# Sample attention of a hybrid decoder step: cached keys turned on VectorE in 32x32 blocks, scores as 32x64 products on eight array tiles, value product moved into the merge

## What is computed

```python
def latent_attention(q_lat, q_rope, c, kr, q_pos, k_pos):
    s = (jnp.einsum('bqhr,bkr->bhqk', q_lat, c)
         + jnp.einsum('bqhp,bkp->bhqk', q_rope, kr)).astype(jnp.float32) * ATTN_SCALE
    s = jnp.where(k_pos[None, :] <= q_pos[:, None], s, -jnp.inf)
    pr = jax.nn.softmax(s, axis=-1).astype(c.dtype)
    return jnp.einsum('bhqk,bkr->bqhr', pr, c)
...
    o = jnp.einsum('bthr,rhv->bthv', o_lat, w_kv[..., QK_NOPE:]).reshape(b, t, MLA_HEADS * V_HEAD)
    y_b = o @ p['w_branch_b']
```

## Time and profile before

| what | value |
|---|---|
| median of 3 runs | 2714.29 us (2712.4 to 2716.27) |
| profiled execution | span 2723.1 us, first to last instruction; no other time of it is recorded |
| PE busy, DVE busy, ACT busy in that span | 92%, 67%, 50% |
| prompt attention ends, sample attention starts | about 251 us |
| first product of the merge | 551.61 us |

### The profile page before, as it was taken

The page is one execution under the profiler, slowest core; times in us unless marked ns, Lnnn a source line. Parts: engine busy times, 40 slices in busy tenths (PEclk is TensorE's granted clock), DMA queues, the critical chain, the costliest instruction groups (busy, mean ns, idle before and its releaser), DMA issues. The chain is left out here.

```text
span 2723.1 us, 35695 instructions
## 1 busy us (share of the span) xinstructions
PE 2506.0 (92%) x12991; PEld 1924.5 (71%) x12991; DVE 1834.4 (67%) x2157; ACT 1354.4 (50%) x1417; POOL 454.7 (17%) x367
## 2 busy tenths in 40 slices
PE   8798999888996999997988899999999999999994
PEld 5355555588994454447976778888888888888883
DVE  0344444343774676563445689999999999999997
ACT  0243322132332454343223377777777777777774
POOL 0001122000001232220011522222111222222211
PEclk9899999898997898898998899999999999999997
DMA  4102344132224134304253699999999999999995
GB/s 145 69 1 99 102 170 155 39 98 77 79 63 138 30 122 126 89 11 112 82 164 131 193 387 396 396 381 381 380 382 382 384 380 376 384 378 378 380 377 183
DMA packets 242307, 585.41 MB, mean 215 GB/s; under 512 B 25632, under 2 KB 114976, under 8 KB 237728
## 3 DMA queue, kind: packets, MB, share of 16 engines
q1 hardware_dynamic: 225176, 508.42, 51.1%
q0 software_dynamic: 17024, 75.53, 9.2%
HBM read 548.10 MB, written 35.67 MB: 214 GB/s over the span
## 5 line engine op out<-in xcount | busy, mean ns | idle before, releaser
L2406 DVE TENSOR_TENSOR w_lo<-w_raw,w_hi 128x2048 fp32r<-128x2048 f32 x291 | 660.2, 2289 | 60.6 <-ACT w_hi L2356 53.8
L2356 ACT ACTIVATE w_hi<-w_raw 128x2048 fp32r<-128x2048 f32 x288 | 550.4, 1916 | 137.7 <-PE banks L2299 102.5
L2299 PE MATMUL banks<-w_hi,x_hi 128*128 128x512 f32 x1024 | 319.9, 394 | 2.4 <-DVEq L2445 2.1
L2299 PE MATMUL banks<-w_lo,x_hi 128*128 128x512 f32 x1024 | 317.0, 391 | 0.0
L2299 PE MATMUL banks<-w_hi,x_lo 128*128 128x512 f32 x1024 | 316.6, 391 | 0.0
L2406 DVE TENSOR_TENSOR w_lo<-mergedT,w_hi 128x2048 fp32r<-128x2048 f32 x96 | 220.1, 2292 | 38.0 <-ACT w_hi L2356 37.9
L2299 PEld LDWEIGHTS banks<-w_hi,x_lo 128*128 128x128 f32 x1024 | 192.9, 188 | 41.0
L2299 PEld LDWEIGHTS banks<-w_lo,x_hi 128*128 128x128 f32 x1024 | 192.8, 188 | 40.8
L2299 PEld LDWEIGHTS banks<-w_hi,x_hi 128*128 128x128 f32 x1024 | 190.7, 189 | 40.5 <-DVEq L2445 2.1
L2356 ACT ACTIVATE w_hi<-mergedT 128x2048 fp32r<-128x2048 f32 x96 | 183.8, 1915 | 34.4 <-PE banks L2299 29.7
L2259 POOL DMA_INDIRECT y_sum<-xT,to_row x32 | 50.9, 1590 | 858.1 <-ACT xT L2388 858.1
(11 more groups left out here) (460 smaller groups left out, 4724.2 us busy)
## 6 DMA issues: line engine op xcount, KB each, us to landing
w_raw<-in_exp_w_gu SPq DMA_DIRECT2D x196, 1024.0 KB, 10.7
w_raw<-in_exp_w_down SPq DMA_DIRECT2D x96, 1024.0 KB, 6.4
mergedT<-in_exp_w_gu SPq DMA_DIRECT2D x64, 1024.0 KB, 10.3
mergedT<-in_exp_w_down SPq DMA_DIRECT2D x32, 1024.0 KB, 10.1
w_x<-in_w_in SPq DMA_DIRECT2D x11, 1024.0 KB
out<-h SPq DMA_DIRECT2D x20, 512.0 KB, 2.6
wz<-in_w_in SPq DMA_DIRECT2D x4, 2048.0 KB, 11.6
dec<-acs_rows SPq DMA_DIRECT2D x16, 512.0 KB, 4.1
```

The source lines that it names most:

```text
L2299: mm = pe.matmul(banks[:, bank + c, :], x[:, k, :], part[:, s % NHI, j, c * 512:(c + 1) * 512], start=start, stop=last)
L2356: act.activation(w_hi[:, s % NHI], raw(s, par), ACT.Copy).then_inc(hi_ready, 1)
L2406: dve.tensor_tensor(w_lo[:, s % NHI], raw(s, par), w_hi[:, s % NHI].bitcast(F32), ALU.subtract).then_inc(lo_ready, 1)
```

## The change

- **Keys.** The 20 PE transposes of a unit and their five copies go. DVE turns the keys itself, in 32x32 blocks, from the ring to `keyT` in SBUF: per unit two transposes of 1024 columns (latent features) and one of 512 (rotary). In `keyT` partition 32i + x then holds feature x of a block of 32 features, for the keys of partition group i.
- **Scores.** A 32-feature block is multiplied by itself: 32 rows of the array (group i) by 64 columns (half c) make a product with 256 keys. Ten blocks, two halves, four groups give 80 products for two units, which now form one step (`PAIRS` = 16 steps). The group i writes to PSUM bank i. The queries must lie on all four groups: SP writes them to DRAM in the stage before (`q_rows`) and reads them back four times per sequence (`q4`).
- **Softmax.** No score copy: DVE takes the maximum of a step from PSUM, ACT takes the exponent from PSUM, with a running maximum and a factor `alpha` that rescales the first step of a sequence when the second is added (`gather`).
- **Pipeline.** One step is behind the scores instead of five units. The ring has nine places, two of which are lent by `wkv`, whose value half SP loads again at the end of the stage.
- **End.** The two halves are added on DVE, with ACT moving one half across partitions; the product with the value half of `wkv` stands in `stage_merge`, where DVE's copies to `oT` come between its `tile_low`.
- **POOL** clears five small tiles after its second unit.

```diff
+            @block.sync
+            def _(sp):
+                sp.wait_ge(prep_out, 4 * HEADS)
+                by_rank = io.q_rows.rearrange("b r j q -> r j b q")
+                for j in range((KVL + ROPE) // 32):
+                    at = slice(32 * (j % 4), 32 * (j % 4) + 32)
+                    q = sb.qlS[at, j // 4] if j < 8 else sb.qrS[at]
+                    sp.dma_start(by_rank[:, j], q.rearrange("p b h t -> p b (h t)")).then_inc(q_put, 16)
+                sp.wait_ge(q_put, 16 * (KVL + ROPE) // 32)
...
-    UNITS = NSEQ * 4
-    RING = 8
+    PAIRS = 2 * NSEQ
+    UNITS = 2 * PAIRS
+    RING = 9
+    LENT = (6, 7)
+    HALF = 2 * P
+    NJ = (KVL + ROPE) // 32
+    PARTS = ((0, 4), (4, 8), (8, NJ))
...
+        keyT = buf("keyT", [P, NJ, 2 * HALF])
+        q4 = buf("q4", [P, 2, NJ, NQ])
+        prob = buf("prob3", [P, 2, BLK * P])
...
+                def queries(b):
+                    for i in range(4):
+                        sp.dma_start(q4[32 * i:32 * (i + 1), b % 2], io.q_rows[b]).then_inc(q_in[b % 2], 16)
+
+                queries(0)
+                queries(1)
+                for b in range(2, NSEQ):
+                    sp.wait_ge(scored[2], 2 * (b - 1))
+                    queries(b)
+                sp.wait_ge(pv_done, PAIRS - 3)
+                w_val = io.wkv.rearrange("(k p) (h d) -> p k h d", p=P, h=HEADS)
+                for r in range(2):
+                    sp.dma_start(sb.wkv[:, r].rearrange("p (h d) -> p h d", h=HEADS)[:, :, NOPE:], w_val[:, r, :, NOPE:]).then_inc(val_in, 16)
+                sp.wait_ge(val_in, 32)
...
+                def turn(n):
+                    b, half = step(n)
+                    pe.wait_ge(expd, n + 1)
+                    for g in range(2):
+                        if n >= 1:
+                            pe.wait_ge(p_out[g], n)
+                        for k in range(4):
+                            at = (4 * g + k) * P
+                            mm = pe.transpose(banks[:, 4 + g, k * P:(k + 1) * P], prob[:, n % 2, at:at + P], K[:, K_ID:K_ID + P])
+                        mm.then_inc(p_ready[g], 1)
...
+                def scores(n):
+                    b, half = step(n)
+                    if n >= 1:
+                        pe.wait_ge(expd, n)
+                    if half == 0:
+                        pe.wait_ge(q_in[b % 2], 64 * (b // 2 + 1))
+                    for part, (first, end) in enumerate(PARTS):
+                        pe.wait_ge(keyed[part], n + 1)
+                        for j in range(first, end):
+                            for c in range(2):
+                                for i in range(4):
+                                    at = slice(32 * i, 32 * (i + 1))
+                                    mm = pe.matmul(banks[64 * c:64 * (c + 1), i, 0:HALF], q4[at, b % 2, j, :], keyT[at, j, c * HALF:(c + 1) * HALF],
+                                                   start=(j == 0), stop=(j == NJ - 1))
+                        mm.then_inc(scored[part], 1)
...
+                def values(n):
+                    b, half = step(n)
+                    if n >= 1:
+                        pe.wait_ge(pv_out, n)
+                    for k in range(BLK):
+                        if k % 4 == 0:
+                            pe.wait_ge(p_out[k // 4], n + 1)
+                        for c in range(2):
+                            mm = pe.matmul(banks[64 * c:64 * (c + 1), 6, 0:KVL], probT[:, n % 2, k, 64 * c:64 * (c + 1)], rows_of(2 * n + c)[:, k, :],
+                                           start=(k == 0), stop=(k == BLK - 1 and (c == 1 or half == 1)))
+                    if half == 0:
+                        pe.wait_ge(fresh_out, b + 1)
+                        mm = pe.matmul(banks[0:NQ, 6, 0:KVL], probT_new[:, b % 2, :], c_new, start=False, stop=True)
+                    mm.then_inc(pv_done, 1)
...
+                fresh()
+                for n in range(PAIRS + 1):
+                    if n >= 1:
+                        turn(n - 1)
+                    if n < PAIRS:
+                        scores(n)
+                    if n >= 1:
+                        values(n - 1)
+                for b in range(NSEQ):
+                    pe.wait_ge(weighed, b + 1)
...
+                def exponents(n):
+                    b, half = step(n)
+                    act.wait_ge(negd, n + 1)
+                    act.activation(prob[:, n % 2].rearrange("p (k i x) -> p i k x", k=BLK, i=4), scores_at.rearrange("p i (k x) -> p i k x", k=BLK),
+                                   ACT.Exp, bias=neg[:, b, half + 1:half + 2], scale=ATT_SCALE, accum_out=part_sum[:, b, half:half + 1]).then_inc(expd, 1)
+                    if half == 0:
+                        act.activation(prob_new[:, b, TS * b:TS * (b + 1)], new[:, b, :], ACT.Exp, bias=neg[0:NQ, b, 1:2], scale=ATT_SCALE,
+                                       accum_out=new_sum[0:NQ, b:b + 1]).then_inc(fresh_expd, 1)
+                    else:
+                        act.activation(alpha[:, b:b + 1], neg[:, b, 1:2], ACT.Exp, bias=neg[:, b, 2:3], scale=-1.0).then_inc(alphad, 1)
...
+                def turn_keys(n, part):
+                    first, end = PARTS[part]
+                    if n >= 1:
+                        dve.wait_ge(scored[part], n)
+                    for c in range(2):
+                        u = 2 * n + c
+                        if u >= AHEAD_UNITS:
+                            dve.wait_ge(unit_in[u % RING], 32 * (u // RING + (u % RING >= AHEAD_UNITS)))
+                        src = rots_of(u) if part == 2 else rows_of(u)[:, :, 32 * first:32 * end]
+                        ins = dve.transpose(keyT[:, first:end, c * HALF:(c + 1) * HALF].rearrange("p j (k x) -> p j k x", k=BLK),
+                                            src.rearrange("p k (j x) -> p j k x", x=32))
+                    ins.then_inc(keyed[part], 1)
...
+                def highest(n):
+                    b, half = step(n)
+                    dve.wait_ge(scored[2], n + 1)
+                    if n >= 2:
+                        dve.wait_ge(negd, n - 1)
+                    dve.reduce_max(mx[:, n % 2:n % 2 + 1], scores_at, mybir.AxisListType.XY).then_inc(maxed, 1)
+                    dve.wait_ge(maxed, n + 1)
+                    if half == 1:
+                        dve.wait_ge(negd, n)
+                    dve.scalar_tensor_tensor(out=neg[:, b, half + 1:half + 2], in0=mx[:, n % 2:n % 2 + 1], scalar=-ATT_SCALE,
+                                             in1=neg[:, b, half:half + 1], op0=ALU.mult, op1=ALU.min).then_inc(negd, 1)
+
+                def gather(n):
+                    b, half = step(n)
+                    dve.wait_ge(pv_done, n + 1)
+                    if half == 0:
                         dve.tensor_copy(o_rows[:, b, :], banks[:, 6, 0:KVL]).then_inc(pv_out, 1)
-
-                dve.wait_ge(expd, NSEQ)
+                    else:
+                        dve.wait_ge(alphad, b + 1)
+                        dve.wait_ge(pv_out, n)
+                        dve.scalar_tensor_tensor(out=o_rows[:, b, :], in0=o_rows[:, b, :], scalar=alpha[:, b:b + 1], in1=banks[:, 6, 0:KVL],
+                                                 op0=ALU.mult, op1=ALU.add).then_inc(pv_out, 1)
...
+                for n in range(PAIRS):
+                    if n >= 2:
+                        gather(n - 2)
+                    if n + 1 < PAIRS:
+                        turn_keys(n + 1, 0)
+                    highest(n)
+                    if n + 1 < PAIRS:
+                        turn_keys(n + 1, 1)
+                        turn_keys(n + 1, 2)
+                gather(PAIRS - 2)
...
-                for h in range(HEADS):
-                    if h >= 2:
-                        pe.wait_ge(o_out, h - 1)
-                    for r in range(2):
-                        mm = pe.matmul(banks[:, 4 + h % 2, 0:NS], sb.wkv[:, r, h * 256 + NOPE:(h + 1) * 256], olS[:, r, h, :],
-                                       start=(r == 0), stop=(r == 1))
...
+                for h in range(HEADS):
+                    if h >= 4:
+                        pe.wait_ge(o_out, h - 3)
+                    for r in range(2):
+                        mm = pe.matmul(banks[:, 4 + h % 4, 0:NS], sb.wkv[:, r, h * 256 + NOPE:(h + 1) * 256], sb.olS[:, r, h, :],
+                                       start=(r == 0), stop=(r == 1))
+                    mm.then_inc(o_ready, 1)
+                pe.wait_ge(o_out, HEADS)
...
                     tile_low(j)
+                    dve.wait_ge(o_ready, j + 1)
+                    dve.tensor_copy(sb.oT[:, j, SEQ:T], banks[:, 4 + j % 4, 0:NS]).then_inc(o_out, 1)```

On PE, in the steady part of the sample attention: first the rows of two units of before (line 647 turns keys, 667 and 672 turn probabilities, 684 and 686 are scores, 698 and 701 values).

```order
L647 MATMUL banks<-const,rows 128x128 x8
L647 MATMUL banks<-const,rots 128x128 x4
L647 MATMUL banks<-const,rows 128x128 x8
```

(53 more changed lines are left out.)

317 lines of the change are left out of this document (102 added, 215 removed).

## The result

The changed kernel takes **2602.1 us** (median of 4 runs, 2592.5 to 2604.7). The kernel before took 2715.3 us beside it (4 runs, 2712.4 to 2720.2). The ratio is 0.9576, with a 95% interval from 0.9548 to 0.9603: 113 us less, faster. The forecast was 2595, in a range from 2578 to 2668.

What follows compares the result with a forecast made beforehand. PE was taken to bound the sample attention, at 9.95 us a step instead of 15.5. Stage end 543.3 - 422.5, less 1.8 in the merge, gives 119 us off 2723.1: span 2604, median 2595 us, range 2578 to 2668.

Steps and rivals of the forecast that it cites:

- The sum: Whole kernel: 119 us off the span of 2723.1 gives 2604; scaled to the median, 2595 us.
- The step: PE in the sample attention, two units: 9.95 us a step, 5.55 less than 15.5.
- Scores: PE, each step: 160 half products on eight parts streaming together, loads queuing across row groups, 4.9 us.
- Values: PE, each step: 32 half products in pairs, 3.65 us, plus 0.2 on average for new rows: 3.85.
- DVE: DVE, each step: transposes 5.7 us at one column a cycle, plus maximum, small operation and gather: about 7.7.
- The order of waits: Steady steps: maximum and exponent take 2.8 us, covered by PE's 3.85 of values; later transposes also covered.
- The start: Stage's first steps: queries until about 256, step 0's scores end near 261, step 1's at about 271.5.
- The end: Sample attention's end: 14 steps lead to 410.8, remaining work ends at about 422.5, against 543.3 before.
- B: PE's supply at 58 ns a pair, or DVE with doubled transposes, too slow: 2661 or 2647 us; chance 0.28.
- C: PE's scores: array parts sharing columns take turns, 17.2 us of scores a step, about 2780 us; chance 0.10.
- D: PE's clock: products of 32 rows might not hold it up; at 1.2 GHz 2741 us; chance 0.03.
- E: Whole kernel: no change to tell, which needs a step of 17.8 us; chance 0.01.

Runs made afterwards that it cites:

- more_dve_4: Changed kernel with four further DVE transposes of 512 columns in each step, ahead of the next step's keys: 2604.9 us.
- late_heads: Changed kernel with two heads' sums per bank and all eight copied out by one instruction behind the gate's low part: 2603.1 us.
- heads_back: Changed kernel with the heads' value products and their copies moved from the merge back to the end of the sample attention: 2610.2 us.
- half_columns: Changed kernel with score products of 128 instead of 256 columns in every step but the first: 2592.7 us in one run.
- four_parts: Changed kernel with the same score products reordered, the array's left-half four parts first, then the right half's four: 2621.73 us in one run.
- part_in_row: Changed kernel with the same score products reordered, four products of one array part in a row before the next part: 2819.34 us in one run.
- no_later_gathers: Changed kernel without the gathers of units 9 to 31, later units reusing the ring's rows: 2597.9 us.

## Why the prediction was right

**The sum.** It was made against the span: 119 us off. In the traces the mark moved by 116.6 us, and the next stage behind the merge (convolution) starts at 549.09 instead of 666.90, 117.8 us sooner. The step that missed is the last one, the scaling to the median: it took the 0.3% (9 us) by which the span of before lay over its median for a property of the kernel, but the span of after (2602.9) is not above its median. 2723.1 - 119 = 2604 was the forecast for a span, and 2602.9 came. That this is met to 1 us is in part luck: the steps came out 4.5 us cheaper than forecast, the start 5.5 us and the end 2.0 us dearer, as worked out below.

**The step: 9.95 us forecast, 9.30 to 9.64 measured**, 9.5 on average without step 1 and without the pause.
- Scores 4.9, measured 4.58. The open price, parts that differ in rows, is nothing: all eight start within 0.05 us and a round is 0.2155, so the ideal 4.3 and 0.3 for the change of form. Loads did not queue across row groups, which I had taken (0.4 dearer).
- Values 3.85, measured 3.51 and 0.52 for the new rows' products in every second step; turning 1.2, measured 1.03.
- Over 14 steps, 136.4 us from start to start (270.85 to 407.27) where 139.3 were forecast: 6.1 us in hand from thirteen shorter steps, less the pause of 2.0 and 1.2 for step 1, which took 11.20 us because half of its scores' time was at the half clock.

**DVE: 7.7 us a step forecast (its terms add up to 7.5), 7.4 measured.** A transpose took 1224 ns for 1024 columns and 670 for 512, thus 1.08 ns a column and 0.12 us fixed, next to 1.04 ns a column of DVE's fp32 operations in the earlier trace rows. With the Trainium skill's rule in Vector Engine (DVE) Microarchitecture Reference, section 3.8 (one element per cycle per lane), the trace agrees. more_dve_4, with 2.9 us more a step, shows that a doubled transpose (5.7 more) would have decided. The order of waits held as well: PE never waits for DVE or for the exponent in the steady part.

**DMA** share 0.70 forecast, 0.72 to 0.76 measured; no steady step waits for a gather.

**The start: step 1's scores end at 271.5 forecast, at about 277 measured** (270.85 and 6.2 us). This term was undersized. Queries were to land at about 256 and came at 260.5 (258 in another execution), the first scores took 6.25 us instead of 4.9 and those of step 1 took 6.20, both in part at the half clock, where 4.57 is the time at the full one. The exponent between them came as forecast in kind, with PE idle for 2.84 us, and behind that idle time the clock fell a second time. The sum had no term for the clock. Together 5.5 us late.

**The end: 422.5 forecast, about 425.5 measured** (DVE's last copy, 424.80 and 0.69). From the end of step 1's scores to the end of the last it was 134.8 us, 4.5 less than forecast, and from there to the stage's end 13.7 instead of 11.7, the chain of gather, move, sum and transposes behind the last product being 2 us longer than I had it: 5.5 - 4.5 + 2.0 = 3.0 us late. From the stage's end to the mark it was 9.5 us where 8.3 + 1.8 were forecast, so the mark came 2.4 us late (435.03 against 432.6) in this execution, and 1.2 early in the other. late_heads puts 1.24 us on the eight copies that were to cost 1.8, and heads_back puts the whole move at 6.2 us gained.

**The rivals.** B, supply: refused by half_columns, at 14 to 19 ns a pair where B had 58. The row of line 1897, 25 ns, was the nearer one. The Trainium skill's 62 ns per product (TensorE: Matmul & The Clock Gate, "Wait — 56ns, not 53.3ns?") is not what these products show. Its 10.6 times on 16 parts ("Measured speedup vs the span model") would have meant, by the prediction's estimate, 6.5 us of scores, and 4.58 came. C, parts that share columns take turns: refused by the kernel after and again by four_parts, where four parts of the same columns start 6 to 7 ns apart. But the price of C is real in another guise: part_in_row has 16.23 us of scores and is 103 us slower than before. The condition is not what the parts share but which order they stand in, and the prediction had no rival for that. D: clock 1.00 in the steady part; but the worry had ground, as part_in_row, with two parts at work, stayed at the half clock for its first two steps (whether for its 32 rows no run shows). E: did not come.

## What to carry to other kernels

When small products go to several array parts, let consecutive products go to different parts, all of them in turn, before a part gets its second one: the same products take 4.2 or 16.2 us from first to last start by order alone, and PE counts as busy throughout in both. By the estimate above one more product may wait at a taken part, and the one after it stops the list. A price that no trace has (here DVE's 32x32 transposes, row groups side by side) can be bounded by the nearest rows of the same engine, and the dense rows told more than the long ones. For edits worth 1 to 3 us of 2600, read a mark in the trace close behind the edit: the remainder of this program moved by up to 6 us from one execution to the next.

## What was not expected of the hardware

- Eight parts start 6.6 ns apart when each gets one product in turn. With longer runs per part the overlap falls, to 5.2 and 5.5 us a step, and at eight pairs in a row to two parts at a time (16.2 us). The estimate of one product waiting per part and 16 unfinished ones fits all four orders within 4%, but is untested.
- PE can be busy without a pause and yet be granted the half clock: in part_in_row for two steps' scores, 31 us each, until 324.94 us.
- One pair of load (64 columns) and product takes no more than 14 ns of supply in the quickest steps of half_columns, less than the 25 ns of the densest row of before.
- Scores of half the width bring ten pauses of "issue" where there was one: when a step's 160 pairs are taken in 2.3 to 3.6 us instead of 4.2, beside gathers at a DMA share of 0.78, PE waits for its list. In all traces such a pause ends 2.2 to 2.9 us after an instruction transfer's start. That the gathers matter for the one pause of the full width is shown by no_later_gathers; how they delay the instructions is open.
- Scores with two sets of sums in the same banks, so that step n + 1 could start before the maximum of n, were not tried.
